# Late modulation in a hybrid trunk layer: two request groups stacked on 64 partitions each, and one two-column sum in place of two one-column ones

## What is computed

```python
def modulation(cvec, w_ada, b_ada):
    m = jax.nn.silu(cvec) @ w_ada + b_ada          # (1024,) @ (1024, 6 * 1024)
    m = m.reshape(m.shape[:-1] + (1, N_MOD, D_MODEL))
    return tuple(m[..., i, :] for i in range(N_MOD))
...
    sh1, sc1, g1, sh2, sc2, g2 = modulation(cvec, w_ada, b_ada)
    x = x + g1 * merge_branches(...)
    h = modulate(x, norm_g[1], sh2, sc2)
    x = x + g2 * moe_ffn(h, ...)
```

## Time and profile before

| | |
|---|---|
| time of three runs | 1177.34, 1178.04 and 1179.57 us, median 1178.04 us |
| span of the profiled execution | 1177.1 us |
| PE busy | 1131.6 us, 96% |
| DVE busy | 910.9 us, 77% |
| ACT busy, POOL busy | 676.9 us (58%), 262.8 us (22%) |
| merge stage | from about 509 to 720 us |
| output projection | from about 723 to 797 us |
| late modulation: loads, DVE, PE | 32 loads of 512 KB, 104.2 + 9.2 us busy, 14.9 us busy |

### The profile page before, as it was taken

The page is one execution under the profiler, slowest core; times in us unless marked ns, Lnnn a source line. Parts: engine busy times, 40 slices in busy tenths (PEclk is TensorE's granted clock), DMA queues, the critical chain, the costliest instruction groups (busy, mean ns, idle before and its releaser), DMA issues.

```text
span 1177.1 us, 20125 instructions
## 1 busy us (share of the span) xinstructions
PE 1131.6 (96%) x7220; PEld 1034.7 (88%) x7220; DVE 910.9 (77%) x1275; ACT 676.9 (58%) x1041; POOL 262.8 (22%) x142
## 2 busy tenths in 40 slices
PE   8999999999999999999999999996999999999996
PEld 5699999999999998899999999995788888888874
DVE  6839797978879797866555555738899999899887
ACT  3656757666766757642222222336688787787753
POOL 0232222122212221133333332211111001111040
PEclk9999999999999999999999999997999999999999
DMA  9326512222121212124444436608899999999995
GB/s 366 124 99 185 169 42 82 73 68 74 52 81 58 80 40 81 41 90 144 143 143 143 143 107 221 232 14 326 335 360 417 430 411 403 417 413 413 427 317 164
DMA packets 54876, 233.27 MB, mean 198 GB/s; under 512 B 5368, under 2 KB 22048, under 8 KB 46368
## 3 DMA queue, kind: packets, MB, share of 16 engines
q1 hardware_dynamic: 50496, 216.79, 49.1%
q0 software_dynamic: 4320, 15.73, 4.0%
HBM read 211.50 MB, written 21.00 MB: 198 GB/s over the span
## 4 chain that ended last, share of the span: by engine, by line
PE 50%; DVE 3%; DMA 1%; ACT 1%; issue 1%; SPq 0%; DVEq 0%; ACTq 0%
PE PS L986 23%; PE PS L751 22%; PE PS L976 1%; PE PS L856 1%; DMA Wg<-in_experts 1%; PE PS L901 1%; PE PS L999 1%; DVE hrow L1883 0%; DMA fgb<-in_final_g 0%; PE PS L947 0%; DVE yo L2148 0%; DVE G L2118 0%; DVE WgLo L2021 0%; PE PS L889 0%; DVE WgLo L2041 0%
## 5 line engine op out<-in xcount | busy, mean ns | idle before, releaser
L621 POOL TENSOR_TENSOR wLo<-wRaw,wHi 128x1024 fp32r<-128x1024 f32 x80 | 202.8, 2536 | 547.1 <-ACT wHi L1110 547.1
L751 PE MATMUL PS<-hHi,wHi 128*128 128x320 f32 x896 | 285.2, 318 | 3.4 <-DVE hLo L1538 2.5
L751 PE MATMUL PS<-hHi,wLo 128*128 128x320 f32 x896 | 277.4, 310 | 0.0
L751 PE MATMUL PS<-hLo,wHi 128*128 128x320 f32 x896 | 277.4, 310 | 0.0
L751 PEld LDWEIGHTS PS<-hHi,wHi 128*128 128x128 f32 x896 | 169.4, 189 | 4.4 <-POOL wLo L621 2.7
L751 PEld LDWEIGHTS PS<-hLo,wHi 128*128 128x128 f32 x896 | 169.1, 189 | 0.0
L751 PEld LDWEIGHTS PS<-hHi,wLo 128*128 128x128 f32 x896 | 168.8, 188 | 0.0
L1707 DVE SCALAR_TENSOR_TENSOR acc<-adaL,csil,acc 128x512 f32<-128x512 f32 x112 | 104.2, 988 | 9.9 <-DMA adaL<-in_w_ada_late 9.4
L1110 ACT ACTIVATE wHi<-wRaw 128x1024 fp32r<-128x1024 f32 x80 | 84.0, 1051 | 46.0 <-PE PS L751 44.7
L2021 DVE TENSOR_TENSOR WdLo<-Wd,WdHi 128x2048 fp32r<-128x2048 f32 x34 | 76.4, 2287 | 13.1 <-ACT WdHi L1337 13.1
L2021 DVE TENSOR_TENSOR WgLo<-Wg,WgHi 128x2048 fp32r<-128x2048 f32 x34 | 76.3, 2286 | 9.7 <-ACT WgHi L1337 9.6
(11 more groups left out here) (365 smaller groups left out, 2827.4 us busy)
## 6 DMA issues: line engine op xcount, KB each, us to landing
wRaw<-in_wtiles SPq DMA_DIRECT2D x80, 512.0 KB, 3.4
Wu<-in_experts SPq DMA_DIRECT2D x18, 2048.0 KB, 9.5
Wg<-in_experts SPq DMA_DIRECT2D x18, 2048.0 KB, 10.6
Wd<-in_experts SPq DMA_DIRECT2D x17, 2048.0 KB, 9.7
adaL<-in_w_ada_late SPq DMA_DIRECT2D x32, 512.0 KB, 4.2
ada<-in_w_ada SPq DMA_DIRECT2D x8, 1024.0 KB, 18.9
slot_rows<-Ys SPq DMA_DIRECT2D x16, 512.0 KB, 10.4
slot_rows<-tab SPq DMA_DIRECT2D x12, 512.0 KB
```

Of the source, the lines that this page charges most:

```text
L621: nc.gpsimd.tensor_tensor(wLo[b][:], wRaw[b][:], wHi[b][:].bitcast(F32), ALU.subtract).then_inc(w_lo, 1)
L751: r = mm(PS[:, bank, 0:HALF], w[:, k, :], x[:, k, cols], start=(k == 0 and w is wHi[b] and x is xh), stop=(k == KT - 1 and w is wLo[b]))
```

## The change

The 1024 rows of the matrix are cut into 16 blocks of 64 rows in place of 8 blocks of 128. A block is loaded twice, to partitions 0 to 63 and to 64 to 127, and `csil` gets columns 8 to 23 in which a block's 64 values for group 0 stand on the lower partitions and those for group 1 on the upper (built on the host from the same inputs, through a `cT` with 24 blocks in place of 8). So one instruction of 128x512 serves both groups for 64 rows, and a chunk has again 16. Odd and even blocks go to two accumulators, `acc[:, 0]` and `acc[:, 1]`, and one more DVE instruction adds them. `ada_sums` then has 4 products whose moving operand is `pair`, two columns with ones on the lower and on the upper partitions.

The loads of a step x are now four of 256 KB in place of one of 512 KB: for both buffers b, two transfers to 64 partitions each. Each step uses both buffers, so the wait of buffer b is on the step just before.

```diff
         def modulation(j, x):
-            wait(sp, adaL_used[x % 2], 2 * j + x // 2)
-            sp.dma_start(adaL[x % 2][:], w_ada_late[bass.ds(j, 1), :, 2 * x:2 * x + 2].rearrange("o p k c -> (o p) k c")) \
-                .then_inc(adaL_in[x % 2], 16)
+            for b in range(2):
+                wait(sp, adaL_used[b], (4 + b) * j + x)
+                for g in range(2):
+                    sp.dma_start(adaL[b][g * HK:(g + 1) * HK],
+                                 w_ada_late[bass.ds(j, 1), :, 4 * x + 2 * b:4 * x + 2 * b + 2]
+                                 .rearrange("o p k c -> (o p) k c")).then_inc(adaL_in[b], 16)
...
         def ada_sums(bank, j):
-            pe.wait_ge(adaL_used[1], 2 * j + 2)
+            pe.wait_ge(adaL_used[1], 5 * j + 5)
             for t in range(ADW // P):
-                for g in range(2):
-                    c = HALF + 2 * t + g
-                    x = mm(PS[:, bank, c:c + 1], acc[:, g, t * P:(t + 1) * P], ones[:, 0:1], start=True, stop=True)
+                c = HALF + 2 * t
+                x = mm(PS[:, bank, c:c + 2], acc[:, 0, t * P:(t + 1) * P], C("pair"), start=True, stop=True)
...
         def ada_piece(j, x):
-            b = x % 2
-            if x == 0:
-                wait(dve, ada_tp, j)
-            else:
-                dve.wait_ge(adaL_used[1 - b], 2 * j + (x - 1) // 2 + 1)
-            dve.wait_ge(adaL_in[b], 16 * (2 * j + x // 2 + 1))
-            for k in range(2):
-                for g in range(2):
-                    w, c1 = adaL[b][:, k, :], csil[:, 2 * x + k, g:g + 1]
...
+            for b in range(2):
+                m = 4 * x + 2 * b
+                dve.wait_ge(adaL_in[b], 32 * (4 * j + x + 1))
+                for k in range(2):
+                    w, c1 = adaL[b][:, k, :], csil[:, KT + m // 2, k:k + 1]
...
+            if x == 3:
+                dve.wait_ge(adaL_used[1], 5 * j + 4)
+                seq.last()
+                v.tensor_tensor(acc[:, 0, :], acc[:, 0, :], acc[:, 1, :], ALU.add).then_inc(adaL_used[1], 1)
```

More of the change, by code:

```diff
@@ L63 @@
 PACK = 4 * P + 2 * P
+HK = P // 2
 def consts():
@@ L81, in consts @@
     c["one16"] = np.ones((P, 16))
+    c["pair"] = (np.arange(P)[:, None] // HK == np.arange(2)[None, :]).astype(np.float64)
     q = np.arange(P)
@@ L130, in build @@
     ones = keep("ones", [P])
-    cvec = keep("cvec", [KT, 2])
-    ctan = keep("ctan", [KT, 2])
-    csil = keep("csil", [KT, 2])
+    cvec = keep("cvec", [2 * KT, 2])
+    ctan = keep("ctan", [2 * KT, 2])
+    csil = keep("csil", [2 * KT, 2])
     bada = keep("bada", [6 * KT, 2])
@@ L1691, in ada_piece @@
         def ada_piece(j, x):
-            b = x % 2
-            if x == 0:
-                wait(dve, ada_tp, j)
-            else:
-                dve.wait_ge(adaL_used[1 - b], 2 * j + (x - 1) // 2 + 1)
-            dve.wait_ge(adaL_in[b], 16 * (2 * j + x // 2 + 1))
-            for k in range(2):
-                for g in range(2):
-                    w, c1 = adaL[b][:, k, :], csil[:, 2 * x + k, g:g + 1]
-                    if x == 0 and k == 0:
-                        y = v.tensor_scalar(acc[:, g, :], w, c1, None, ALU.mult)
-                    else:
[L1705 to L1708, removed]
+            for b in range(2):
[3 more added lines that the diff above has]
+                    w, c1 = adaL[b][:, k, :], csil[:, KT + m // 2, k:k + 1]
+                    if m == 0:
+                        if k == 0:
+                            wait(dve, ada_tp, j)
+                        y = v.tensor_scalar(acc[:, k, :], w, c1, None, ALU.mult)
+                    else:
+                        if k == 0:
+                            seq.last()
+                        elif b:
+                            dve.wait_ge(adaL_used[0], 4 * j + x + 1)
+                        else:
+                            dve.wait_ge(adaL_used[1], 5 * j + x)
+                        y = v.scalar_tensor_tensor(acc[:, k, :], w, c1, acc[:, k, :], ALU.mult, ALU.add)
+                    if k:
                         y.then_inc(adaL_used[b], 1)
@@ L1765, in _ @@
         with nc.vector.Fori(0, KT // 2 - 2) as jj:
-            seq.enter(jj, 2 * 12)
+            seq.enter(jj, 2 * 8)
             merge(2 * jj + 2, 0, 8 * jj + (N1 + 12))
@@ L2223 @@
         "xT": columns(x).transpose(0, 2, 1),
-        "cT": columns(cc).transpose(0, 2, 1),
+        "cT": np.concatenate([columns(cc).transpose(0, 2, 1), np.concatenate(
+            [x.reshape(KT, 2, HK).transpose(2, 0, 1) for x in cc], 0)], 1),
         "w_ada": arr("w_ada")[0, :, 0:2 * D].reshape(KT, P, -1, ADA).transpose(2, 1, 0, 3),
-        "w_ada_late": arr("w_ada")[0, :, 2 * D:].reshape(KT, P, -1, ADW).transpose(2, 1, 0, 3),
+        "w_ada_late": arr("w_ada")[0, :, 2 * D:].reshape(2 * KT, HK, -1, ADW).transpose(2, 1, 0, 3),
         "b_ada": np.repeat(arr("b_ada")[0].reshape(6 * KT, P).T[:, :, None], 2, 2),
```

## The result

The changed kernel takes 1203.12 us (four runs, 1198.23 to 1209.26); the kernel before, run beside it, 1178.80. The ratio is 1.0201, with a 95% interval of 1.0171 to 1.0231: about 24 us slower, where 11 were forecast, and outside the range. The profiled execution spans 1201.6 us.

The account below looks back on a forecast made before the run. PE, busy for 96% of the span, was taken to bound the kernel. The terms -4.2 - 1.7 + 8.25 + 6.3 + 2.5 = +11.2 us, set on the median of 1178.04, gave 1189 us, range 1180.5 to 1199.5.

Parts of the forecast that it names:

- near waits: Loads wait for DVE's step just before: weight tiles in merges late by 8.25 us together, sums of chunk 6 by 6.3.
- Removed, 5.9 us: Halved sums on PE save 4.2 us in merges 1 to 5, nothing in merge 6, 1.7 us in the output projection.
- Price of a pair, 4.45 us: Time from first issue to data for two 64-partition loads: 4.07 us of one load plus some 0.38 for the second issue.
- The upper bound, 5.65: What a pair of loads would take, in us, if halves hold each other up as whole loads do.
- rival 1: Halves hold each other up: 5.65 us per pair, more waiting in merges and chunks 6 and 7; +20.8 us, 1199; chance 0.18.
- Merges 1 to 5, 1.3 us each: PE waits 1.3 us per merge for weight tile T(j+1,0), whose load stands behind step 1's loads; 6.5 us together.
- Merge 0, 1.75 us: PE waits 1.75 us: weight tile ready at 539.45, wanted at 537.69, with no shorter sums to save there.
- clock gain: Low-clock drops behind both sums of the output projection could vanish, a gain of 3.2 us; no gain was counted.
- Chunk 6, 6.3 us: Output projection: PE's sums wait 6.3 us because DVE's chain of load and work ends at 744.7, asked for at 738.4.
- Chunk 7, 2.5 us: Output projection: PE waits 2.5 us more, as ACT rounds out tile 5 late behind DVE's last step and residual addition.
- "No row shows such a transfer.": The prediction's remark that no profile row showed a 64-partition transfer, made when pricing the pair and in rival 1.

Follow-up runs that it names:

- e3: The changed kernel with one load to 128 partitions in place of each pair to 64, same bytes, waits and buffers; 1191.17 us, ratio 1.0094.
- e1: The kernel before with 4 two-column products per call of the sums, all on the first accumulator, loads and DVE work unchanged; 1172.63 us, ratio 0.9946.
- e7: The changed kernel with the first 1 MB of Wg loaded behind out tile 5's weights, not ahead of chunk 7's steps 2 and 3; 1204.20 us.
- e9: The changed kernel with two further buffers in the merges, so loads there wait for the step two back; 1191.24 us, ratio 1.0096.
- e5: The kernel before with its loads and waits, sums stacked through csil columns and one fold per chunk on DVE; 1176.14 us, ratio 0.9958.
- e12: e9 with two further buffers in chunks 6 and 7 too, so loads there also wait two steps back; 1182.90 us, ratio 1.0012.
- e6: The kernel before with each 512 KB load cut into two to 64 partitions, same bytes and waits; 1180.40 us, ratio 0.9995.
- e2: The kernel before with each step loading one 128-row block into both buffers, waiting for the step just before, old sums; 1186.79 us, ratio 1.0057.
- e10: e9 with each buffer filled by one 512 KB load to 128 partitions in place of the pair; 1184.79 us, ratio 1.0041.

## Why the prediction was wrong

The sign and the mechanism (near waits hold up a weight tile and the sums) were right, and so were the places but for the one in chunk 7; the size was too small by more than half. Three steps failed: the price of a pair, which was taken from a single load (4.45 us, measured 4.6 to 5.5); the clock, which was put at nothing where PE's new waits lower it (2.6 us in merge 1, and the 1.7 us saved on the late sums); and chunk 7, whose loads were priced without the 1 MB of Wg ahead of them (2.5 us forecast). e3, with one load in place of the pair, measures 12 us above the kernel before, near the 11.2 forecast for the change; its parts differ (A +1.9, B +8.6), so that is in part luck. By the prediction's steps:

- **Removed, 5.9 us.** Right for PE left alone: 4.4 us in A of e1 (4.2 forecast), and 1.8 in B without the clock. In the changed kernel only the part in the merges was had; the 1.7 us of the late sums were not, since they ran at half clock behind PE's waits. The prediction also says that no low clock follows the sums in a merge: it does in merge 6 (15.85 us for 96 products in the earlier trace rows), which it overlooked, and that drop is missing in the changed kernel's profile (-1.5).
- **Price of a pair, 4.45 us.** Mis-sized: from first issue to use 5.0 us in merge 3, and in chunk 6 4.6 to 5.5 (733.0 to 738.45 for the longest). I took the price of the nearest 512 KB load plus 0.38; the issues alone take 0.47 to 0.60 us each where 0.33 was assumed. The upper bound, 5.65, was nearer, and rival 1 (halves that hold each other up, 1199) was the best of the cases. In the Trainium skill the page "SBUF — State Buffer", section "Can I just issue two DMAs to hit both halves?", states that two such transfers run one after the other. The rows agree in direction: in merge 3 and chunk 6 the pair took 4.6 to 5.5 us where one load of the same 512 KB took 3.5 to 4.8 in e3; that is far from twice.
- **Merges 1 to 5, 1.3 us each.** Too high for merges 3 to 5, where the wait is 0.6 to 0.9 us: POOL now comes behind DVE's step 0 (626.09 against 625.37), so the 2.91 us of the earlier trace rows is 1.40, while the weight lands 0.65 us later than assumed. Too low for merges 1 and 2, 2.1 and 2.4 us, where POOL still held DVE up (two instructions of step 0 took 3.57 us at 562.58, one 2.91 at 594.61).
- **Merge 0, 1.75 us.** 3.6 us: the weight took 6.42 us to land, not the 5.0 assumed. This is the term that did damage beyond itself, since the low clock behind it took 2.6 us more in merge 1. I had looked for a clock gain and never for a clock loss from my own waits. The size differs between executions: in e7, with the same merges, the tile lands after 5.01 us, T(1,0) is 2.2 us late, and the low clock behind it costs 1.6. A together: forecast 8.25 - 4.2 = +4.05, found +8.3.
- **Chunk 6, 6.3 us.** Mis-sized, and by luck the stretch came right: T(6,0) to the sums is longer by 6.4, but PE waits 7.8 us, and 1.5 came back in merge 6. From DVE's start on the chunk to the end of its addition it takes 24.2 us, 22.9 forecast: the pairs took longer, while POOL stood less in the way.
- **Chunk 7, 2.5 us.** The step that failed most: 5.2 us of waiting and 1.3 of low clock behind it. I gave its loads the 4.45 us of a quiet queue and left the 1 MB of Wg out of the list of what is issued ahead of steps 2 and 3 (9.02 and 6.11 us). I also named the rounding of out tile 5 as the late thing; it was the router's product ahead of the sums. e7 shows that the megabyte delays the loads, but not that moving it saves anything.
- **"No row shows such a transfer."** True, but the stretch that decided was not the transfer. Far waits hid pairs of 5.9 us (e9).
- The clock in the routing (the last 1.7 us) and in the attention (the first 1.7 us) are no terms of the change. That they differ because of it is not shown.

Open: why the clock behind chunk 6 stays low in e5, whose sums are as short as those of e1 and only some 1.5 us later (PE is idle for 1.7 us ahead of them, in e1 not at all); and how much of what e12 has left is volume and how much the pairs.

## What to carry to other kernels

Before doubling the bytes or cutting a transfer, ask how far ahead its buffer is freed: in the merges splitting, and double volume, cost nothing with the wait two steps back (e6, e9), while in the output projection, where the queue is full, the doubled and split loads did cost (e12); with the wait one step back they cost some 12 us (the change against e3) and 11 (e3 against e2, its shorter sums added), since every microsecond of a load then stands in front of whatever the queue holds next. List everything issued ahead of a load in each stage, for a stage with its own large transfers needs its own price. And if a stacked layout is wanted for its consumer, look for a way to fold the result once at the end, rather than to load the source twice.

## What the runs showed of the hardware

- Transfers to 64 partitions occupy the DMA engines longer for the same bytes. From 585 to 670 us, e9 (pairs) and e10 (one load), with the same bytes of the late modulation in 48 loads or in 24:

```profile
585.00:670.00 85.00, 85.00 (x586) 85.00 (x585) 60.23 (x75) 19.09 (x29) 31.35 (x12) 1.00 0.84 218
```

```profile
585.00:670.00 85.00, 85.00 (x587) 85.00 (x587) 61.06 (x74) 18.71 (x29) 30.10 (x12) 1.00 0.64 222
```

  A DMA share of 0.84 against 0.64 at 218 and 222 GB/s. It fits the 6 us that the pair costs in the output projection at equal volume, where the queue has no room.
- SP takes 0.47 to 0.60 us to issue such a transfer in the changed kernel; one to 128 partitions takes 0.33 to 0.43 in the kernel before, and 0.34 to 0.58 in the changed one, where it stands behind those.
- PE's idle time of 3.6 us at T(1,0) was followed by half the granted clock; those of 2.1 and 2.4 us at T(2,0) and T(3,0) were followed by nothing of the kind (14.35 us for the next 96 products). The length of the idle time doesn't decide it alone: in e7 2.1 us at T(1,0) were followed by half clock, and so were 1.7 us between small products in e5 (739 to 741 us, granted 0.50). e7:

```profile
543.00:545.00 2.00, 2.00 (x10) 2.00 (x9) 1.05 (x2) 1.06 (x1) 0.00 (x0) 0.50 0.39 131
```

- Vector instructions whose output stands on the other 64 partitions (e5's fold) took 0.75 us for 64x512, about the price of 128x512 in place (0.70).
